# Other planner costs: the instruction order of a fused encoder layer on eight cores

## The reference, cut to what matters

```python
h = x @ w_in[l]                                       # 8 blocks of 1024 columns
u, v, q, f_pre, i_in, og, g_a, g_b = jnp.split(h, splits, axis=-1)
y_a = sgu_mixer(gelu(u), gelu(v), ...)                # u * (W_s layer_norm(v) + b), blocks of 128 positions
y_b = hgrn2_mixer(q, f_pre, i_in, og, ...)            # 8 heads, a recurrence over chunks of 64 positions
merged = sigmoid(g_a) * (y_a @ w_branch[l, 0]) + sigmoid(g_b) * (y_b @ w_branch[l, 1])
x = layer_norm(ALPHA * x + merged @ w_out[l], ln1_g[l], ln1_b[l])
ffn = (gelu(causal_dwconv(x @ w_gate)) * (x @ w_val)) @ w_down   # hidden width 2816
ple = sigmoid(x @ ple_w_gate[l]) * (p[l] @ ple_w_proj[l])
x = layer_norm(ALPHA * x + ffn + ple, ln2_g[l], ln2_b[l])
```

## Time and profile before

| | |
|---|---|
| median of 3 runs | 2753.15 us (2749.62 to 3078.89) |
| the profiled execution | 2753.4 us |
| its span, slowest core | 2751.8 us (cores: 2720.2 to 2751.8) |
| busy: PE, DVE, ACT, POOL | 2482.8, 1742.1, 1580.2, 213.1 us |
| mean granted clock of PE, slowest core | 0.969 |

### The profile page before, as it was taken

One profiled execution on the slowest core, in us unless ns is written; L12 is line 12 of the kernel. 1 busy time (PEld: TensorE's weight loads), 2 busy tenths in 40 slices (PEclk: granted clock), 3 DMA queues, 4 the chain that ended last, 5 costly groups with the idle time before them and its releaser, 6 DMA issues.

```text
span 2751.8 us, 44104 instructions; the slowest of 8 cores (2720.2 to 2751.8 us)
## 1 busy us (share of the span) xinstructions
PE 2482.8 (90%) x13666; PEld 1247.7 (45%) x13666; DVE 1742.1 (63%) x3043; ACT 1580.2 (57%) x2351; POOL 213.1 (8%) x567
## 2 busy tenths in 40 slices
PE   6887899978899989999999989999899998999797
PEld 4443444433445444454445444454444544454343
DVE  3865774637566486575865577654876658655654
ACT  4764774626755377472866367663785447743452
POOL 2101121001210001000100000000010000100010
PEclk9999999998999999999999999999999999999898
DMA  9979676796897757766345544544345463435243
GB/s 175 189 142 170 115 137 125 174 197 169 172 186 179 209 154 201 182 183 199 123 131 146 188 138 139 148 155 168 124 138 155 143 204 108 131 107 188 100 154 115
DMA packets 119749, 430.52 MB, mean 156 GB/s; under 512 B 13280, under 2 KB 13408, under 8 KB 119520
## 3 DMA queue, kind: packets, MB, share of 16 engines
q1 hardware_dynamic: 90000, 324.13, 35.7%
q0 software_dynamic: 29520, 103.56, 24.4%
HBM read 471.94 MB, written 59.24 MB: 193 GB/s over the span
## 4 chain that ended last, share of the span: by engine, by line
PE 64%; DMA 14%; ACT 10%; issue 6%; DVE 4%; POOL 0%; ACTq 0%; DVEq 0%; SPq 0%; POOLq 0%
PE pg L563 57%; DMA sb_wsl<-w_in 4%; PE pg L601 2%; DMA sb_wsl<-scr_win 2%; PE pg L764 2%; DMA sb_wsl<-w_up 1%; DVE sb_resid L716 1%; DMA sb_wsl<-w_o 1%; DMA sb_xbf<-xT 1%; ACT sb_gs L865 1%; DMA scr_win<-sb_wsl 1%; ACT sb_t32b L869 1%; DMA scr_wug<-sb_wsl 1%; PE pg L892 1%; ACT L693 1%
## 5 line engine op out<-in xcount | busy, mean ns | idle before, releaser
L563 PE MATMUL pg<-sb_xbf,sb_wsl 128*128 128x512 bf16 x6400 | 1482.2, 387 | 156.4 <-DMA sb_wsl<-w_in 38.3
L563 PEld LDWEIGHTS pg<-sb_xbf,sb_wsl 128*128 128x128 bf16 x6400 | 622.5, 99 | 917.1 <-issue 247.8
L563 PE MATMUL pg<-sb_arena,sb_wsl 128*128 128x512 bf16 x1408 | 312.0, 379 | 1.3 <-DMA sb_wsl<-w_dn 1.3
L814 DVE SCALAR_TENSOR_TENSOR sb_t32a<-sb_t32a,pg 128x512 f32<-128x512 f32 x96 | 65.9, 688 | 236.6 <-PE pg L563 233.6
L563 PEld LDWEIGHTS pg<-sb_arena,sb_wsl 128*128 128x128 bf16 x1408 | 136.7, 98 | 163.4 <-issue 3.6
L871 DVE SCALAR_TENSOR_TENSOR sb_t32b<-sb_gs,sb_cst,sb_t32b 128x512 f32<-128x512 f32 x176 | 131.9, 749 | 121.5 <-ACT sb_t32b L869 119.0
L808 ACT ACTIVATE sb_t32a<-pg 128x512 f32<-128x512 f32 x96 | 56.6, 597 | 223.4 <-PE pg L563 208.0
L865 ACT ACTIVATE sb_gs<-pg 128x512 f32<-128x512 f32 x176 | 104.0, 591 | 133.8 <-PE pg L563 126.3
L882 DVE TENSOR_TENSOR sb_arena<-pg,sb_t32b 128x512 bf16<-128x512 f32 x176 | 121.1, 689 | 67.6 <-PE pg L563 63.2
L866 POOL COPY sb_cy<-sb_gs 128x2 f32<-128x2 f32 x176 | 56.1, 319 | 1352.6 <-ACT sb_gs L865 1352.3
L666 DVE SCALAR_TENSOR_TENSOR sb_sh<-sb_sh,sb_el,pd 128x128 f32<-128x128 f32 x384 | 131.5, 343 | 36.9 <-PE pd L654 25.7
(11 more groups left out here) (149 smaller groups left out, 3306.6 us busy)
## 6 DMA issues: line engine op xcount, KB each, us to landing
sb_wsl<-scr_win SPq DMA_DIRECT2D x196, 512.0 KB, 4.2
sb_wsl<-scr_wug SPq DMA_DIRECT2D x66, 512.0 KB, 3.9
sb_wsl<-w_in POOLq DMA_DIRECT2D x60, 512.0 KB, 10.9
sb_wsl<-w_up POOLq DMA_DIRECT2D x55, 512.0 KB, 7.1
sb_wsl<-scr_wuv SPq DMA_DIRECT2D x55, 512.0 KB, 3.6
sb_wsl<-scr_wdn SPq DMA_DIRECT2D x40, 512.0 KB, 3.8
scr_win<-sb_wsl SPq DMA_DIRECT2D x32, 512.0 KB, 9.0
sb_resid<-xT SPq DMA_DIRECT2D x32, 512.0 KB, 7.7
```

The lines of the kernel that those rows point to most:

```text
L563: last = e.matmul(out, lhsT=slot[:, k * 256 + j * 128:k * 256 + (j + 1) * 128], rhs=rhs3[:, k0 + k, :], start=(k0 + k == 0), stop=(k0 + k ...
L814: fw.dve([TH, v], [TH], lambda e, v=v, th=th: e.scalar_tensor_tensor(out=th, in0=th, scalar=1.0, in1=v.ap[:], op0=ALU.add, op1=ALU.mult), ...
```

## The change

Six numbers change: the costs by which the planner sets the order. An ACT operation of 512 columns is taken as 0.692 us where it was 0.557; one of DVE gets 0.03 us more (0.723 for 0.693); issuing a DMA costs SP 0.36 us for 0.07 and POOL 1.1 for 1.0; and three single operations get widths that stand for another duration. Operations, buffers, keys and the PE costs are as before.

```diff
     def act(self, ins, outs, fn, n=512, ptrs=0, tset=None):
-        return self._record("act", ins, outs, fn, 0.13 + n / 1200.0 + 0.093 * ptrs, tset)
+        return self._record("act", ins, outs, fn, 0.265 + n / 1200.0 + 0.093 * ptrs, tset)
 
     def dve(self, ins, outs, fn, n=512, cost=None):
-        return self._record("dve", ins, outs, fn, cost if cost is not None else 0.16 + n / 960.0)
+        return self._record("dve", ins, outs, fn, (cost if cost is not None else 0.16 + n / 960.0) + 0.03)
...
     def dma(self, q, dsem, ins, outs, fn, nbytes, after=()):
-        return self._record(q, ins, outs, fn, 0.07 if q == "sp" else 1.0, None,
+        return self._record(q, ins, outs, fn, 0.36 if q == "sp" else 1.1, None,
...
-                        out=kb[64:128], in_=pt.ap[64:128, 0:512].rearrange("p (b c) -> p b c", c=128)), n=300)
+                        out=kb[64:128], in_=pt.ap[64:128, 0:512].rearrange("p (b c) -> p b c", c=128)), n=256)
...
-                    op0=ALU.mult, op1=ALU.add), n=700)
+                    op0=ALU.mult, op1=ALU.add), n=622)
...
-                    op0=ALU.mult, op1=ALU.add), n=300)
+                    op0=ALU.mult, op1=ALU.add), n=367)
```

## The result

The changed kernel is slower: 2833.41 us in the median of four runs (2793.30 to 3066.85) beside 2754.46 for the kernel before in the same comparison. Some runs of either kernel are longer because one die has a lower clock; ratios and comparisons leave them out, and the others (2793.30 to 2806.00 us here) stand at **1.0175** times those of before (95% interval 1.0141 to 1.0209), some 48 us. The profiled execution took 2804.05 us, its span 2802.4. The forecast was 2758 with a range of 2718 to 2800: the median lies outside it, and the runs that the ratio uses stand around its upper end, with a median of 2802.

What follows compares the result with a forecast made beforehand. PE was taken as the bound in most of a tile, the DVE and ACT chain at the norm, weight loads in the first tiles. From 2753.4 us, -18.7 + 3.5 + 3.0 + 6.9 + 5.1 + 1.8 + 3.4 = +5.0 gave 2758, range 2718 to 2800.

Steps and rivals of the forecast that it cites:

- Place 1: Banks emptied by L869: 13 places of quick reuse fall to 4, recurring waits mostly go, a gain of 18.7 us.
- The list of kinds: Recurring PE waits for L869 in the timeline, of 2.48, 1.55, 1.36, 1.33 and 1.28 us, summed to 21.9 us.
- The two small terms: Banks behind DVE operations L882 and L643 retaken at once in more places: losses of 3.5 and 3 us.
- Place 2: Gating of tiles 1, 4, 5 and 6: PE idles for one projection more, 1.73 us each, a loss of 6.9 us.
- first rival: Filling work is spent early, norms idle longer, half of it again lost to the clock: about 2780 us, chance 0.22.
- Place 3: First norm: longer DVE work and less PE filling work cost 5.1 us, a late evacuation L582 another 1.8.
- the 1.8: First norm, tiles 4 to 6: first gate projection's bank waits for L582, now behind all eight L837; three times 0.6 us.
- Place 4: Weight loads: SP's missing cover falls, POOL's rises in the first tiles; a loss of 3.4 us, up to 13.
- The second: Waits for ACT go at large, 60 us faster: 2695 us, chance 0.08 in full and 0.05 in part.
- The third: First tiles' loads: eight loads with under 6 us of cover make PE wait longer; about 2815 us, chance 0.10.

Runs made afterwards that it cites:

- e15: Kernel before, with the first gate projection moved behind the eighth L791 in the gating of tiles 4, 5 and 6: 2761.14 us, 1.0042.
- e17: Changed kernel, gate projection moved (tiles 4 to 6), L768 moved forward (four tiles), mean products L707, L709 put ahead of a projection (tiles 4 to 6): 2781.03 us, 1.0084.
- e7: Changed kernel with gate projection moved between fifth and sixth L791 (tiles 1, 4, 5, 6) and L768 moved forward (four tiles): one usable run, 2791.87 us, no ratio.
- e6: Changed kernel, two L768 evacuations moved from behind eight L917 to behind the first and third, in four late tiles: 2787.53 us, 1.0126.
- e14: Kernel before with all of the change's costs for the operations of tiles 0 to 2 only: 2769.24 us, 1.0076.
- e16: Kernel before with VectorE costs 0.03 us lower, plus gate projection and L768 moved in tiles 4, 5 and 6: 2749.75 us, 1.000.

## Why the prediction was wrong

**Place 1, the banks behind L869: right in what it counted, wrong as a gain.** It was to bring 18.7 us, and by the list it brought 28.2. But in a late tile the end of a norm is set by the chain over DVE and ACT, and PE's idle time there is the chain's length less the PE work left for it. Windows of tile 5 from L711 to the first L865, and on to the fourth; before:

```profile
1950.10:1966.80 16.70, 11.41 (x45) 4.85 (x45) 16.12 (x30) 14.76 (x22) 0.00 (x0) 0.80 0.18 61
1966.80:1982.20 15.40, 12.40 (x79) 7.07 (x80) 11.49 (x24) 8.90 (x15) 1.48 (x6) 0.89 0.13 39
```

and after:

```profile
1993.90:2011.00 17.10, 8.22 (x35) 3.28 (x35) 16.32 (x30) 15.65 (x22) 0.00 (x0) 0.80 0.09 31
2011.00:2021.50 10.50, 8.86 (x70) 5.27 (x68) 9.19 (x21) 8.82 (x13) 0.92 (x5) 1.00 0.18 51
```

The second window lost 5 us of length, and the waits for L869 with it. The first has ten matmul records fewer, and PE idles there for 8.9 us instead of 5.3. By the matmuls in them, PE had 7.8 + 10.6 us of work at full clock in the two windows, and now has 6.1 + 8.3: they are 4.5 us shorter with 4.0 us less work. Their loss is 13.6 us before and 13.3 after; the medians of the cores went from 12.2, 12.7 and 13.6 in tiles 4 to 6 to 13.3, 13.3 and 13.6. So in these tiles the wait for L869 went into other waits of the same chain, above all the three for L716 (17.4 us), which stand at the ends of these norms. The waits for L837 (+7.0) are in the first three tiles. The step that failed is the subtraction of 18.7 us from the end: a wait behind a chain was counted as if the chain didn't set the end. Only the B stretches show a gain, 4.7 us in the late tiles. (The list of kinds also left out three waits of 1.50 us for L869, so more was there than the 21.9 us counted. The two small terms came as priced, as waits: L882 +3.8 for 3.5, L643 +3.1 for 3.0.)

**Place 2, the gating: the right place and direction, half the size, and mostly another cause.** Priced at 1.73 us of idle time a tile; by the medians it costs 3.5 to 4.1 in the changed kernel and 3.5 to 3.9 in e15, where in tile 4 0.8 is idle time and the rest clock. The term left the clock at nothing. The prediction had the clock's number for the norm (0.84) and used it in its first rival only.

**Place 3, the first norm.** Forecast +5.1 and +1.8. The third edit of e17 shows that one projection ahead of L707 had its part (13.1 us off R, where gating and L768 had given 11.9 in e7, and 8 off B against e7). The terms' size wasn't measured singly; the waits for L582, for which the 1.8 stood, fell from 16.9 to 9.6 us.

**Place 4, the loads.** Forecast +3.4, bound 13. The waits for `w_in` rose by 12.0 us, but others fell, and all loads together rose by 4 on the slowest cores. By the medians of the six complete cores they went from 86 to 99, but to 81 in e6 and 88 in e17, which have the same order ahead of tile 3. So the term can't be told from the difference between one profile and the next. e14 puts 21 us on the new costs of tiles 0 to 2; how much of this is loads, and how much gating and norms of those tiles, stays open, for no run changed a load's cover alone.

**What was left out.** The evacuations L768 behind the second norm had no term. Moving them gave 7.9 us in the R stretches of tiles 4 to 6 (e6). The prediction named the gap itself (what queues behind what on ACT); a walk along ACT's order would have shown eight L917 in a row.

**What it comes to.** In the R stretches of tiles 4 to 6, which lose 30 us, the sum had three times 1.73 for the gating and little else. The gating's clock and the L768 are shown by edits, and the three edits of e17 take back 13 us there. The other 17, and the 8 to 20 us ahead of tile 3, have no shown cause. The range's lower end was not worked out rightly either: the sum with 26 us gained and half of the losses is 2739, not 2718.

**The rivals.** The first came nearest to the time (2780 for some 2802), and its mechanism, idle time with as much again lost to the clock, is that of the R stretches. But it was put at the norms: there PE idles longer in the first window (8.9 us for 5.3) with the clock at 0.80 in both kernels, while the clock's loss stands in the gating. That work of `h_stage` was spent early is not shown beyond the one projection of e17. The second fell: nearly all of L869's waits went and nothing came of it (all waits for ACT were 98 us, not some 90). The third did not happen by its own sign: waits for `w_in`, `w_up` and `w_dn` came to 54 us where it named 80. The late tiles, forecast at 325 to 328 us, took 332.

## What to carry to other kernels

A wait that goes away in a list of waits is a gain only if nothing else sets the end of that stretch; price an order stretch by stretch, as length less the work put into it, before believing a wait. In a static plan, truer costs need not give a faster order: 0.03 us on VectorE's costs (with three widths) moved the time by 1.4%, and 0.035 off ScalarE's by 0.9%, both for the worse. Walk each engine's fixed order for long rows of work that nobody waits for (eight L917) with something behind it that the matmul engine needs, and keep a matmul group inside every stretch where another engine sets the pace: here three moved projections cost 11 us, and 60 positions gave back half of a 48 us loss.

## What the runs showed of the hardware

In the gating of tile 5 the full clock was lost with no halt over 1.48 us: PE had five halts of 0.28 to 1.48 us within 6 us, and the window 1900 to 1910 has 0.66 granted, 1.2 GHz for most of its length, though PE was busy for 6.9 of 10 us. With one more projection of 1.73 us between the halts, the stretch kept 1.00 before the change in two tiles of three. The Trainium skill (TensorE: Matmul & The Clock Gate, section What's actually happening) has the same two levels and calls the low one the default, which activity lifts; the trace of the changed kernel has these two levels and no other. The Trainium skill (Perfetto Trace Analysis, section Matmul Optimizations) advises back-to-back matmuls in batches, because the engine scales its power with its utilization; e15 puts a number on it, 2.6 us of clock for 0.8 us of idle time.

Cores that run the same order on the same chip differ by 32 to 41 us (2720.2 to 2751.8 in the profiled run before, 2704.7 to 2745.8 in e16's), nearly as much as the change itself.
